# An MoE decoder trunk on one core: each partition takes two neighbouring rows of an expert's down weights

## The reference, cut to what matters

```
scores = sigmoid(xf @ w_router)                 # 64 experts, top 8 of 4 groups
hdn    = silu(xb @ w_gate[e]) * (xb @ w_up[e])  # w_gate, w_up: 1024 x 256
y      = hdn @ w_down[e]                        # w_down: 256 x 1024
out    = segment_sum(y * gate) + shared expert
```

## Time and profile before

| | us |
|---|---|
| median of three runs | 1737.88 |
| lowest and highest run | 1737.51, 1742.16 |
| span of the profiled execution | 1734.9 |
| PE busy in it | 1608.6 (93%) |
| weight loads (PEld) busy | 1084.3 (62%) |
| DVE, ACT, POOL busy | 399.5, 269.2, 173.4 |

### The profile page before, as it was taken

How to read it: one execution, slowest core, us unless ns; L and a number is a source line. 1 busy time by engine, 2 the same in 40 slices (tenths; PEclk the granted TensorE clock), 3 DMA queues, 4 the chain that set the end, 5 groups by cost and what they waited for, 6 DMA issues and landing times. The chain is left out here.

```text
span 1734.9 us, 26996 instructions
## 1 busy us (share of the span) xinstructions
PE 1608.6 (93%) x10382; PEld 1084.3 (62%) x10382; DVE 399.5 (23%) x1242; ACT 269.2 (16%) x614; POOL 173.4 (10%) x192
## 2 busy tenths in 40 slices
PE   8999899999999999999699998999999999999994
PEld 6676475666656665666476755666666666666663
DVE  1622331121121112111316233311111111112113
ACT  1243101111110111111113421011111111111111
POOL 1112200000000000000212022000000000000002
PEclk9997899999999999999889978999999999999997
DMA  9421428998997899896282305399898879889840
GB/s 334 179 98 62 185 113 337 368 367 343 367 365 298 333 367 369 345 369 242 98 287 96 125 25 196 124 368 369 342 368 358 350 289 369 355 358 366 351 193 25
DMA packets 97562, 470.73 MB, mean 271 GB/s; under 512 B 9328, under 2 KB 13552, under 8 KB 64096
## 3 DMA queue, kind: packets, MB, share of 16 engines
q1 hardware_dynamic: 85040, 442.19, 64.3%
q0 software_dynamic: 11856, 25.55, 4.2%
q10 hardware_dynamic: 608, 2.23, 0.3%
HBM read 484.48 MB, written 3.28 MB: 281 GB/s over the span
## 5 line engine op out<-in xcount | busy, mean ns | idle before, releaser
L544 PE MATMUL bank<-ring,region 128*64 128x256 f32 x4096 | 480.9, 380 | 1.9 <-issue 1.9
L544 PEld LDWEIGHTS bank<-ring,region 128*64 128x64 f32 x4096 | 297.9, 137 | 168.5 <-issue 36.5
L510 PEld LDWEIGHTS bank<-region 128*128 128x128 f32 x1584 | 258.7, 190 | 77.5 <-issue 55.2
L510 PE MATMUL bank<-region 128*128 128x272 f32 (+8 forms) x1584 | 299.0, 332 | 1.5 <-ACT region L948 1.5
L572 PE MATMUL bank<-ring,region 128*64 128x512 f32 x1024 | 248.0, 605 | 0.0
L1490 POOL DMA_INDIRECT region<-h_rows,rank_i x68 | 67.5, 993 | 1159.1 <-DVE rank_i L1177 1134.4
L621 PE MATMUL bank<-hT,ring 128*128 128x272 f32 (+1 forms) x704 | 170.4, 400 | 3.2 <-issue 2.1
L948 ACT ACTIVATE region<-bank 128x512 f32<-128x512 f32 x128 | 76.5, 598 | 541.3 <-PE bank L572 541.3
L621 PEld LDWEIGHTS bank<-hT,ring 128*128 128x128 f32 (+1 forms) x704 | 132.9, 192 | 34.7 <-issue 4.3
L572 PEld LDWEIGHTS bank<-ring,region 128*64 128x64 f32 x1024 | 62.1, 136 | 86.9 <-issue 73.1
L1176 DVE COPY region<-bank 128x2 f32<-128x2 f32 x68 | 10.8, 159 | 405.2 <-PE bank L487 405.2
(11 more groups left out here) (170 smaller groups left out, 1057.1 us busy)
## 6 DMA issues: line engine op xcount, KB each, us to landing
ring<-in_w_down_dram SPq DMA_DIRECT2D x64, 2048.0 KB, 7.6
ring<-in_w_gate_dram SPq DMA_DIRECT2D x64, 2048.0 KB, 9.7
ring<-in_w_up_dram SPq DMA_DIRECT2D x64, 2048.0 KB, 10.4
ring<-in_w_in_dram SPq DMA_DIRECT2D x8, 2048.0 KB, 13.9
ring<-in_w_o_dram SPq DMA_DIRECT2D x4, 2048.0 KB, 14.6
ring<-in_w_in_dram SPq DMA_DIRECT2D x2, 1824.0 KB, 8.9
ln_par<-in_ln_g_dram POOLq DMA_DIRECT2D x4, 512.0 KB, 5.4
ln_par<-in_ln_b_dram POOLq DMA_DIRECT2D x4, 512.0 KB, 7.0
```

Of the source, the lines that this page charges most:

```text
L510: last = mm(bank[b][:, c:c + n], y_sb[:, u, d * 128:(d + 1) * 128], selg[:, u, t:t + n], start=opens and b not in opened, stop=stop, skip_ ...
L544: last = mm(bank[5][64 * e:64 * e + 64, part * F:(part + 1) * F], xgT[:, u, kk, 64 * e:64 * e + 64], w[:, e, kk, :], start=(kk == 0), stop ...
```

## The change

The down weights of an expert are laid out so that partition p holds rows 2p and 2p+1, which are neighbours in memory. A load is then two runs of 8192 bytes to a partition, and its destination view is the one of gate and up. To match, block j of the turn of `h` takes the columns 2p+j, which is every second column of `h`, where it took 128 neighbouring ones. The views that L572 multiplies with, and all counts of instructions, stay.

```diff
-        down_v = a["w_down"].rearrange("l (q e) (j p) n -> (l q) p (e j) n", e=2, p=128)
+        down_v = a["w_down"].rearrange("l (q e) (p j) n -> (l q) p e (j n)", e=2, j=2)
...
-                if part < 2:
-                    src = src.rearrange("o p e n -> (o p) e n")
-                    dst = ring[:, s, :].rearrange("p (e n) -> p e n", e=2)
-                else:
-                    src = src.rearrange("o p e n -> (o p) e n")
-                    dst = ring[:, s, :].rearrange("p (e n) -> p e n", e=4)
+                src = src.rearrange("o p e n -> (o p) e n")
+                dst = ring[:, s, :].rearrange("p (e n) -> p e n", e=2)
...
+                        h_rows_of = mo["h"].rearrange("s (p j) -> s j p", j=2)
                         for j in range(2):
-                            last = pe.transpose(bank[7][:, j * 128:(j + 1) * 128], mo["h"][:, j * 128:(j + 1) * 128], ident)
+                            last = pe.transpose(bank[7][:, j * 128:(j + 1) * 128], h_rows_of[:, j, :], ident)
```

## The result

| | us |
|---|---|
| median of 20 runs, changed kernel | 1743.88 (1738.01 to 1748.19) |
| median of 20 runs, kernel before | 1737.87 (1734.87 to 1744.18) |
| ratio, with its 95% interval | 1.0027 (1.0016 to 1.0038) |
| span of the profiled execution | 1746.4 (before 1734.9) |

The changed kernel is slower by 0.27%, between 2.8 and 6.6 us of 1737.87. That is small, but the interval leaves out 1, and the median lies 1.4 us above the range that I gave. The medians are 6.0 us apart, the means of the same runs 5.0: 13 of the 20 runs of before lie between 1734.87 and 1739.56 us and 7 between 1741.65 and 1744.18, and its median falls among the lower ones.

What follows compares the result with a forecast made beforehand. TensorE's fixed 18.30 us pair was taken to bound the kernel, not the loads. Loads, issue and turn summed to 0 on the 1734.9 us span; with the median 3.0 us above it, the forecast was 1737.9 us, range 1735.0 to 1742.5.

Steps and rivals of the forecast that it cites:

- the range that I gave: Whole kernel: the median was forecast to lie between 1735.0 and 1742.5 us.
- The bound: Expert pairs: TensorE sets the fixed 18.30 us step, since a pair without any load takes as long.
- the loads: Down weight loads on the SP queue: 8 KB runs land as a gate load does, worth 0 on the end.
- the prediction's estimate of under 2 parts in 100: Down load transfers: saving of one 8 KB run against two of 4 KB, from packet and descriptor overheads.
- The place of the cost: Turn of h on TensorE, behind the wait for VectorE: a longer turn is not hidden and is paid 64 times.
- by nearness: Turn of h: stride 2 taken to cost 0, being nearer to stride 1 (140 ns) than to 8 (200 ns).
- The term that the sum had at 0: Turn of h in each pair: the added cost of reading every second column, put at 0 us.
- The rule that supported it: SBUF reads of the turn's weights: 16-byte lines let float32 be strided up to 4 for free, so stride 2 costs 0.
- The upper end: Turn of h: at most 0.03 to 0.05 us more a pair, as the second weight load hides; 3.2 us at most.
- the same sum: Turn of h: two strided turns, 0.55 - 2 x 0.12 = 0.31 us, against 0.28 us for two contiguous ones.
- The fitting rival: First weight load of L561: strided turns cost as at stride 8, 1.9 to 3.2 us, 1739.8 to 1741.1; chance 0.11.

Runs made afterwards that it cites:

- load_alone: Changed kernel with the turn of h contiguous as before, so only the down loads in 8 KB runs differ from before: 1741.04 us against 1740.33, ratio 1.0004.
- turn_alone: Kernel before with only the turn of h reading every second column, loads still in 4 KB runs: 1745.24 us against 1740.33, ratio 1.0033.
- first_strided: Changed kernel with only the first of the two turns of h reading every second column: 1746.85 us in one execution.
- second_strided: Changed kernel with only the second turn of h reading every second column: 4144 us in one execution with further rounds, step 18.31 us in layer 0.

## Why the prediction was wrong

*The bound and the loads were right.* A pair without a load as long as one with many was taken to mean that transfers don't reach the end. load_alone bears it out: its step is that of before to 0.01 us, and its time lies between 1.9 us under and 3.5 us over. The down load, whose cost was read from the gate load of the same shape, landed as that row had it. Its packets took a little less of the DMA engines: over the nine kernels of one round each, the queue's share times the span is 1115.5 to 1116.2 us in the three with runs of 4 KB and 1103.3 to 1108.7 us in the six with 8 KB, an estimate of some 0.14 us less for each of the 64 loads. That is near the prediction's estimate of under 2 parts in 100 of 7.6 us, and nobody waited for it.

*The place of the cost was right.* Of all edits only the turn of `h` was put on TensorE's path, uncovered and paid 64 times, and that is where the 4.2 us are.

*The step that failed is the value taken for it:* "I take 0, by nearness: a stride of 2 is nearer to 1 than to 8". The two rows gave a value at stride 1 and a value at stride 8. I read a line through them, where the runs show a step: 206 ns at stride 2, 207 at stride 4, 200 at 8. The term that the sum had at 0 is 0.066 us a pair, 64 x 0.066 = 4.2 us, as turn_alone shows. Nearness along an axis says nothing unless something shows that the cost moves gradually along it, and two points can't. With ends of 0 and 0.05 us and a shape unknown, the cheap end should not have had 0.80 of the chance against 0.11.

*The rule that supported it.* The Trainium skill's note on cachelines (the page "SBUF — State Buffer", section "Door 1: The DMA port swizzle") has float32 strides of up to 4 for free. Its second half agreed with the 200 ns at stride 8, and I let that lend weight to the first half, which no row showed. The runs contradict it for the weight load of a float32 turn: 66 ns more at a stride of 2, 67 at 4. The measurement decides.

*The upper end was somewhat low.* It said 0.03 to 0.05 us a pair, since only the first weight load would be exposed; the pair paid 0.066. first_strided gives 0.057 for that one, so the idea was nearly right and the price low, and second_strided 0.006 for the one that I had as wholly hidden. Part of the miss is the distance of 0.12 us between later turns, which I worked out with a mean length. Taken singly in the trace of before, the four matmuls of the second group end 0.31, 0.42, 0.53 and 0.64 us after its start, so they are 0.11 apart. With that the same sum gives 0.55 - 2 x 0.11 - 0.28 = 0.05 us. The fitting rival ended at 1741.1 for that reason and would have had 1742.1, which lies inside the range that I gave and still 1.8 us under the measured median. So the mis-sized step alone would not have taken the median out of the range. Of the 1.8 us, 1.0 is the difference between medians (6.0 us apart) and means (5.0 apart) of the two sets of 20 runs. The cause of the other 0.8 us is open: it may be chance, or the stretch between the layers.

*The range was too narrow for a second reason.* The three runs shown lay between 1737.51 and 1742.16, the twenty measured later between 1734.87 and 1744.18, and in other sets of runs the median of the very same kernel was 1740.33 and 1740.16. A spread read from three runs is too small, and a bound of 1742.5 that adds the stride to their lower end left no room for it.

## What to carry to other kernels

Where an engine bounds the kernel and works in a fixed step, look for what each edit adds behind its waits, and multiply by the number of steps: here 66 ns became 4 us. An engine's own record can shorten by more than the time it gives back: 424 ns of weight loads were worth 100 ns. When a layout has to be sorted somewhere, do it in an instruction of an engine that waits anyway, not in the operand of the engine that sets the pace. Subtract the repeated step of two traces, not their spans. And a price known at two sizes may be a step between them: give its dear end the weight until a row at the size in question is there.

## What the runs showed of the hardware

- The weight load of a float32 turn of 128 columns takes 140 ns (turns of `h`) or 147 (turns of tokens) from neighbouring columns, and 206 ns at a stride of 2 columns, 207 at 4 and 200 at 8: a step, not a slope.
- Behind a wait the first strided weight load costs 57 ns of time, the second 6 ns; in the two groups of four, 424 ns of shorter records were worth 100 ns.
- ScalarE's copy of 1024 float32 elements read at a stride of 8 took 2.0 us, against 1.15 us for a square of 1024 neighbouring ones; the two differ in function too. VectorE's product of 256 elements, one operand in PSUM, took 0.61 us with its output written out of order, against 0.42.
- With the down loads in runs of 8 KB in place of 4 KB the packets of the weight queue took some 9 us less of the 16 DMA engines' time over the kernel, of 1116. Here nobody waited for it.
- The stretches outside of the pairs come in two lengths each: ahead of the first copy about 259 us at a granted clock of 0.91 or 262 at 0.90, between the layers about 283.5 at 0.88 or 288.3 at 0.87. The pairs, at 1.00, repeat to 0.01 us.
